# Turning half of the attention output between the last two value products

## The reference, cut to what matters

```python
mix = concatenate([o_a, o_b, o_c, o_d], axis=-1)     # 256 x 1024: A, B, C, D, 256 columns each
x = x + rmsnorm(mix @ w_out, g_post_mix)
```

## Time and profile before

| | us |
|---|---|
| median of 3 runs | 1979.17 (1978.88 to 1979.22) |
| the profiled execution | 1976.11 |
| its span, first to last instruction | 1974.3 |
| PE busy in it | 1897.8 (96%) |
| mean granted TensorE clock | 0.979 of full speed |

### The profile page before, as it was taken

How to read it: one execution, slowest core, us unless ns; L and a number is a source line. 1 busy time by engine, 2 the same in 40 slices (tenths; PEclk the granted TensorE clock), 3 DMA queues, 4 the chain that set the end, 5 groups by cost and what they waited for, 6 DMA issues and landing times.

```text
span 1974.3 us, 23117 instructions
## 1 busy us (share of the span) xinstructions
PE 1897.8 (96%) x9135; PEld 1562.0 (79%) x9135; DVE 1175.4 (60%) x1368; ACT 886.3 (45%) x1071; POOL 83.3 (4%) x100
## 2 busy tenths in 40 slices
PE   7988999999899999999999999998999999999997
PEld 5877888877778888888877778887888877778885
DVE  5775554657765547456566575446556566574555
ACT  5544444555454445344345434443344355444442
POOL 6300000021100000000000000000000000000000
PEclk9988999999799999999999999999999999999998
DMA  8423555544656555654455754557563455645552
GB/s 256 142 65 113 173 189 180 196 157 135 90 173 193 189 173 208 210 189 151 144 170 175 238 174 147 183 183 242 180 222 114 152 184 189 220 156 177 185 187 89
DMA packets 194385, 340.17 MB, mean 172 GB/s; under 512 B 9342, under 2 KB 59422, under 8 KB 194304
## 3 DMA queue, kind: packets, MB, share of 16 engines
q1 hardware_dynamic: 189072, 327.76, 49.8%
q0 software_dynamic: 5232, 11.29, 3.1%
HBM read 333.24 MB, written 5.77 MB: 172 GB/s over the span
## 4 chain that ended last, share of the span: by engine, by line
PE 85%; DVE 7%; ACT 3%; DVEq 2%; issue 2%; DMA 0%; SPq 0%; ACTq 0%
PE G L647 19%; PE G L648 18%; PE G L652 18%; PE T L700 5%; PE A L647 4%; PE A L648 4%; PE A L652 4%; PE G L662 2%; PE G L663 2%; PE G L668 2%; DVE wlo L1605 1%; PE T L749 1%; PE A L662 1%; ACT whi L1155 1%; PE A L759 1%
## 5 line engine op out<-in xcount | busy, mean ns | idle before, releaser
L1605 DVE TENSOR_TENSOR wlo<-raw,whi 128x2048 fp32r<-128x2048 f32 (+3 forms) x300 | 630.0, 2102 | 570.6 <-ACT whi L1155 570.4
L1155 ACT ACTIVATE whi<-raw 128x2048 fp32r<-128x2048 f32 (+3 forms) x300 | 527.1, 1759 | 588.1 <-PE G L652 513.1
L647 PE MATMUL G<-whi,XH 128*128 128x512 f32 (+1 forms) x1408 | 560.1, 398 | 7.6 <-DVE XL L1619 6.3
L648 PE MATMUL G<-whi,XL 128*128 128x512 f32 (+1 forms) x1408 | 549.5, 390 | 0.0
L652 PE MATMUL G<-wlo,XH 128*128 128x512 f32 (+1 forms) x1408 | 346.2, 388 | 0.0
L647 PEld LDWEIGHTS G<-whi,XH 128*128 128x128 f32 x1408 | 266.1, 189 | 64.3 <-DVE XL L1619 8.0
L648 PEld LDWEIGHTS G<-whi,XL 128*128 128x128 f32 x1408 | 266.2, 189 | 53.9 <-issue 1.9
L652 PEld LDWEIGHTS G<-wlo,XH 128*128 128x128 f32 x1408 | 263.9, 188 | 53.6
L700 PE MATMUL T<-ident,arena 128*128 128x128 f32 x804 | 118.6, 288 | 23.0 <-ACT arena L1155 17.3
L700 PEld LDWEIGHTS T<-ident,arena 128*128 128x128 f32 x804 | 97.8, 148 | 42.1 <-ACT arena L1155 17.9
L1155 ACT ACTIVATE arena<-T 128x512 f32<-128x512 f32 (+2 forms) x92 | 46.1, 550 | 159.2 <-PE T L700 159.2
(11 more groups left out here) (237 smaller groups left out, 2240.1 us busy)
## 6 DMA issues: line engine op xcount, KB each, us to landing
raw<-in_w_in SPq DMA_DIRECT2D x112, 1024.0 KB, 7.2
raw<-in_w_mlp_up SPq DMA_DIRECT2D x32, 1024.0 KB, 5.3
raw<-in_w_mlp_down SPq DMA_DIRECT2D x32, 1024.0 KB, 4.9
raw<-in_w_ffn_gate SPq DMA_DIRECT2D x44, 512.0 KB, 3.7
raw<-in_w_ffn_up SPq DMA_DIRECT2D x44, 512.0 KB, 4.8
raw<-in_w_ffn_down SPq DMA_DIRECT2D x44, 512.0 KB, 3.7
raw<-in_w_out SPq DMA_DIRECT2D x16, 1024.0 KB, 4.9
raw<-in_w_ret_proj SPq DMA_DIRECT2D x16, 1024.0 KB, 5.0
```

The costliest lines, as they stand in the source:

```text
L647: nc.tensor.matmul(dst(m), hx[:, k0 + k, rows], hi[:, k, :], start=first and k == 0, stop=False)
L648: nc.tensor.matmul(dst(m), lx[:, k0 + k, rows], hi[:, k, :], start=False, stop=False)
L1155: return nc.scalar.activation(out_, in_, func, **kw)
L1605: tt(lo_, raw[:, slot, 0:n], hi.bitcast(F32), ALU.subtract).then_inc(part_sem(blk, c, s_lo, s_lo1), 1)
```

## The change

PE issues the turn of the A and B half between the value products of job 8 and job 9, as soon as job 7's output is there; the first output unit then stands right behind the last value product. The wait for all ten outputs moves behind that unit. DVE takes the `turn_lo` of that half ahead of `outputs` of job 9, and the squares, sum and mean of C's norm move from behind the jobs to step 9 (C's last job is job 6). ACT takes its root for that norm ahead of `turn_hi` of the half instead of behind it. No instruction is added or removed; both layers of the first block have it.

```diff
@@ constants
+MIX_AB = 1 + max(q for q, job in enumerate(JOBS1) if job[0] in "AB")
@@ PE, beside(q, logits_made)
                     elif q == Q_TURN_D + 1:
                         pe.wait_ge(s_tfree.sem, s_tfree.at(0, L, T_JOB + job_banks(JOBS1, Q_TURN_D)))
+                    elif q == len(JOBS1) + 1:
+                        pe.wait_ge(s_o.sem, s_o.at(0, L, MIX_AB))
+                        turn(0, L, 0, T_MIX, Z[:, :, MIX0:MIX0 + DM], UK)
 
                 run_jobs(0, L, JOBS1, T_JOB, logits1, PR, beside)
 
-                pe.wait_ge(s_o.sem, s_o.at(0, L, len(JOBS1)))
-                turn(0, L, 0, T_MIX, Z[:, :, MIX0:MIX0 + DM], UK)
                 pe.wait_ge(s_tfree.sem, s_tfree.at(0, L, T_MIX + 2))
                 unit(0, L, 0, U_OUT, XH, XL, 0, UK, COLS, bank_pair(1), True, False)
 
+                pe.wait_ge(s_o.sem, s_o.at(0, L, len(JOBS1)))
                 pe.wait_ge(s_mix.sem, s_mix.at(0, L, 1))
                 turn(0, L, 0, T_MIX + 2, Z[:, :, MIX0 + UK * P:MIX0 + DM], UK)
@@ ACT, behind the jobs
+                root(0, L, 2, 1, 8)
                 turn_hi(0, L, 0, T_MIX, UK, XH)
-                root(0, L, 2, 1, 8)
                 hi(0, L, 0, U_OUT + 2)
@@ DVE, run_jobs
                     if 1 <= q <= len(jobs):
                         copy_turned(blk, L, q - 1, jobs, t0, dst)
+                    if q == len(jobs) + 1:
+                        turn_lo(blk, L, 0, T_MIX, UK, XH, XL)
                     if q >= 2:
                         outputs(blk, L, q - 2, jobs)
                     if beside:
@@ DVE, the first block
+                def squares():
+                    dve.drain()
+                    tt(CS, CO, CO, ALU.mult)
+                    dve.drain()
+                    nc.vector.tensor_reduce(stat[:, 0, 1, :], CS.rearrange("p m h d -> p (m h) d"), AX.X, ALU.add)
+                    dve.drain()
+                    mean(1, 8, HD).then_inc(s_ms.sem, 1)
+
                 def beside(q):
+                    if q == 9:
+                        squares()
                     if q == 0:
                         lo(0, L, 0, 13)
...
                 run_jobs(0, L, JOBS1, T_JOB, PT, beside)
-                turn_lo(0, L, 0, T_MIX, UK, XH, XL)
-
-                dve.drain()
-                tt(CS, CO, CO, ALU.mult)
-                dve.drain()
-                nc.vector.tensor_reduce(stat[:, 0, 1, :], CS.rearrange("p m h d -> p (m h) d"), AX.X, ALU.add)
-                dve.drain()
-                mean(1, 8, HD).then_inc(s_ms.sem, 1)
                 invert(0, L, 2, 1, 8)
```

## The result

The changed kernel took 1965.73 us (median of 4 runs, 1961.76 to 1968.02); the kernel before, with it, 1979.03 (4 runs, 1976.94 to 1979.22). The ratio is 0.9933, 95% interval 0.9917 to 0.9949: 13.3 us faster. The forecast was 10.7 us faster, 1968.5, with a range from 1966.0 to 1974.5.

A forecast was written before the change was run, and what follows sets the result against it. PE, busy 96% of the span, was taken as the bound. Gaps and clock together gave 6.3 us in layer 0 plus 4.5 in layer 1, 10.8 off 1979.17: 1968.4, rounded to 1968.5, range 1966 to 1974.5.

The forecast's parts named there:

- The gaps: PE around the A and B half's turn: 1.00 and 1.41 us idle go, gaining 2.8 and 3.15 us by layer.
- Covers: Turn's wait, split, C's squares and ACT's root hide under other work at cost 0; split has 0.4 us to spare.
- The clock: Clock rises before or stays up under the output unit; with the gaps, 6.3 us in layer 0, 4.5 in layer 1.
- The rule on transposes: PE turns do not count as busy work for the clock gate, so the sum would be 5.9 us.
- rival 3: Both layers: gaps alone gain, clock returns only under the output unit; 5.9 us, 1973.3; chance 0.2.

The follow-up runs named there:

- the two fully filled kernels: Small unread matmuls in PE's gaps ahead of job turns: added to the change, 1957.77 us; to the kernel before, also around the mix turn, 1962.34 us.

## Why the prediction was wrong, point by point

**The gaps: right.** "Gain 2.8 us" and "3.15 us", 5.9 in all; with the clock held in both kernels it is 3.05 to 3.22 in layer 0 and 3.16 to 3.33 in layer 1, 6.2 to 6.5 in all. Closing the first gap alone leaves the second (ratio 0.9976 against 0.9954 beside it). In the profiled execution the unit came 5.6 and 4.9 us sooner behind the turn of the probabilities, because the slow clock went with the gaps.

**Covers: right.** The turn waited for nothing; squares and root cost nothing (0.9993 alone, 0.17 us once in the trace); the split was hidden with 0.05 us left where 0.4 was forecast (it ended 1.62 us behind the turn and not 1.41, with job 8's `outputs` ahead of it on DVE, and the unit follows the products with an overlap of 0.16 that the 1.83 us left out); the norm of C was 2.9 us early; everything behind kept its distance.

**The clock: right in kind, mis-sized, and this is the step that failed.** The step is "I let it rise when four slow products, the turn and four more are done: 151.0 + 0.8 + 1.76 + 0.8 = 154.3". It took the fall at 151 from the one trace of before as given. In the profiled execution after the change there was no fall: the turn and all products ran at 2.4 GHz and the unit came 4.48 us behind the turn of the probabilities, not 6.07. Layer 0 gave 7.9 us and not 6.3, layer 1 7.0 and not 4.5. In the forecast's sum the clock stood for 10.8 - 5.9 = 4.9 us; of the 13.3 measured about 7 are left for it once the gaps are taken off. But that is the trace of the fastest run. In the profiled execution of the change when it was run again the clock did fall, at the same place, and the forecast picture of layer 0 is there almost to the tenth:

```profile
152.07 1.09 PE L702 MATMUL T<-ident,arena 128*128 128x128 f32 x8 [2.35 <-ACT arena L1158]
153.00 1.46 PE L761 MATMUL A<-arena 128*128 128x64 f32 x8
154.25 1.92 PE L702 MATMUL T<-ident,arena 128*128 128x128 f32 x8
155.96 2.30 PE L761 MATMUL A<-arena 128*128 128x64 f32 x16
158.07 0.48 PE L649 MATMUL G<-whi,XH 128*128 128x512 f32 x1
```

6.00 us from the first to the last of these starts (forecast 6.07), the clock down within the first products, up again within the second, and the unit at full pace. By the same stretches as in the table above this trace gains 6.4 us in layer 0 and 4.0 in layer 1, 10.4 where 10.8 was forecast, and that group of runs gave 1968.37 against the 1968.5 forecast. So the picture was a fair one of one kind of execution; which kind a median meets was not controlled, and that the later median lies 0.1 us from the forecast is in part luck. This trace also shows what the range left out. Its span is only 7.8 us shorter than that of before, because it reaches the turn of job 9's probabilities 2.5 us later (152.07 against 149.53); part of that is a spell ahead of all that the change touches, from 112.8 to 115.6, where the granted clock is 0.50 here and 1.00 in the trace of before.

**The range: too narrow by that.** I gave 1.5 us for slow matmuls that may move. The 64 executions of the kernel before that were taken beside the experiments lie between 1973.1 and 1981.9, on mean clocks from 0.984 down to 0.976. Taking 2 x (1 - clock) x span as the time at 1.2 GHz in each, a straight line through them has a slope of 0.29 us for each us at the slow level, with a correlation of 0.90. The time at the slow level was 65 us on average in the four runs of the change on record and 69 in the five later ones, against 84 to 88 before. So of 13.3 us about 6.2 are the gaps, shown with the clock held; the other 7 are put down to the clock by subtraction, and the line would give about 6 (an estimate). In the later runs (8.9 us) what is left is 3, and the line would give about 4. The two intervals overlap (0.9917 to 0.9949, 0.9941 to 0.9967). Which execution gets which spell of slow clock was not controlled. Nor is the mean clock all of it: three of the runs on record had 0.982 or 0.983, like all five later ones, and took 1965.6 to 1968.0 where those took 1968.1 to 1969.0. Why the runs on record were the better ones stays open, and with them why the median fell just outside the range.

**The rule on transposes.** In the rows just shown the clock rose with nothing behind it but turns and value products, as in the earlier trace rows; it did so too in layer 1 of this trace, and in both layers of the trace with the turn moved alone. By the rule of the Trainium skill (TensorE: Matmul & The Clock Gate, Part 4: PE-mode transpose) the turns should have added nothing; rival 3, which stood on it, would have given 1973.3 and is out, since in all four cases the clock was up before the unit. But the prediction's own ground, "a mixture like the one behind which it rose in layer 1", does not hold in general either. In layer 1 of the change in layer 0 alone 8 turns and 24 value records follow each other at the slow pace with nothing idle between (531.18 to 538.16, shown above), and the clock did not rise; nor did it in layer 1 with the squares moved alone or with only the first gap closed, which have the same two rows. What separates these from the four that rose is not shown, and what turns by themselves do was not tried.

## What to carry to other kernels

Independent work put between two small dependent matmul groups can pay three times where the clock is in play: the wait before it, the wait behind it, and the pace of the dense matmuls that follow. Price the gaps from the trace, but a trace is one execution: take the clock's share as a distribution over executions, with the scatter of the unchanged kernel as the least width of the range. Where PE has to wait, filling the wait with small matmuls into an unused half of a PSUM bank gave more here (10.6 us on top of the change) than the reordering (8.9 us beside it); and a transfer that nobody needs soon belongs where the loads are idle, not where they are consumed at once.

## What was not expected of the hardware

With small bf16 matmuls of 256 columns, about 0.11 us each, in PE's gaps of 1.0 to 2.35 us the granted clock stayed at 1.00 from 118 to 158 us, where the kernel before has 0.50 from 121 to 137 and again from 151 to 164. Whether the scatter falls with it is not shown: 1.9 and 1.1 us lie between the highest and lowest run of the two fully filled kernels (4 and 5 runs) and 7 us for the kernel before beside them (17 runs), but only 0.9 us for the change without filling (5 runs). Beside three copies of 1.5 MB each, of which the last landed after 71 us, a 1 MB load landed in 26.8 us, and in 5.5 us with the copies moved away.
